# Gating and normalising the probabilities before their transposes, instead of the products after them, in a two-layer attention decoder step

## What is computed

```python
def masked_softmax(logits, valid, sink=None):
    ...
    e = jnp.exp(logits - m)
    den = jnp.sum(e, axis=-1, keepdims=True)
    if sink is not None:
        den = den + jnp.exp(sink - m)
    return e / jnp.where(den > 0, den, 1.0)

def a_finish(x, o, z, gate, w_out):
    n, t = x.shape[:2]
    return x + gate * ((o.reshape(n, t, HD) * jax.nn.silu(z)) @ w_out)

def b_finish(x, o_cmp, o_sel, o_win, z, gl, gate, w_out):
    ...
    mix = jnp.sum(jax.nn.sigmoid(gl)[..., None] * ob * jax.nn.silu(z), axis=2)
    return x + gate * (mix.reshape(n, t, HD) @ w_out)
```

## Time and profile before

| | us |
|---|---|
| runs | 1698.52, 1699.68, 1703.47 |
| median | 1699.68 |
| span of the profiled execution | 1699.8 |
| TensorE matmuls, busy | 1588.0 (93%) |
| VectorE, busy | 934.7 (55%) |
| ScalarE, busy | 613.7 (36%) |
| GpSimd, busy | 485.8 (29%) |

### The profile page before, as it was taken

One profiled execution on the slowest core, in us unless ns is written; L12 is line 12 of the kernel. 1 busy time (PEld: TensorE's weight loads), 2 busy tenths in 40 slices (PEclk: granted clock), 3 DMA queues, 4 the chain that ended last, 5 costly groups with the idle time before them and its releaser, 6 DMA issues.

```text
span 1699.8 us, 31847 instructions
## 1 busy us (share of the span) xinstructions
PE 1588.0 (93%) x11936; PEld 1425.7 (84%) x11936; DVE 934.7 (55%) x2396; ACT 613.7 (36%) x1356; POOL 485.8 (29%) x294
## 2 busy tenths in 40 slices
PE   4579999999699997899999999999999999998997
PEld 1478888888599997788998989989899898886897
DVE  3635555555645415555555755657556575578556
ACT  3413333333214414224434344344443444444112
POOL 0232412221841315355121121211212112149661
PEclk9689999999799997999999999999999999999999
DMA  9233333232612134501021130211101111033732
GB/s 329 92 92 106 106 106 106 107 106 88 236 67 75 47 136 124 141 26 35 15 64 35 29 84 17 88 35 29 35 17 38 35 29 35 18 84 104 255 145 100
DMA packets 82594, 145.16 MB, mean 85 GB/s; under 512 B 19170, under 2 KB 54146, under 8 KB 82274
## 3 DMA queue, kind: packets, MB, share of 16 engines
q1 hardware_dynamic: 69210, 128.64, 23.1%
q10 hardware_dynamic: 10288, 8.46, 1.6%
q0 software_dynamic: 2944, 6.04, 1.3%
HBM read 128.96 MB, written 19.35 MB: 87 GB/s over the span
## 4 chain that ended last, share of the span: by engine, by line
PE 86%; DVE 4%; DMA 3%; ACT 3%; issue 2%; SPq 2%; ACTq 0%; DVEq 0%
PE PS L1032 15%; PE PS L1034 15%; PE PS L1033 15%; PE PS L1287 11%; PE PS L1300 10%; PE PS L1267 5%; PE PS L1268 4%; PE PS L1406 2%; PE PS L1277 2%; DMA WR<-w_ada 2%; PE PS L1229 1%; DMA WR<-sw_v 1%; PE PS L1296 1%; PE PS L1249 1%; PE PS L1382 1%
## 5 line engine op out<-in xcount | busy, mean ns | idle before, releaser
L1032 PE MATMUL PS<-HT_r,WR_r 128*128 128x344 f32 x1344 | 448.8, 334 | 20.0 <-DVE XT_r L1823 15.3
L1034 PE MATMUL PS<-HT_r,WR_r 128*128 128x344 f32 x1344 | 433.4, 322 | 0.0
L1033 PE MATMUL PS<-XT_r,WR_r 128*128 128x344 f32 x1344 | 433.2, 322 | 0.0
L669 POOL TENSOR_TENSOR WR_r<-WR,ONE 128x1024 fp32r<-128x1024 f32 x60 | 116.6, 1943 | 1042.6 <-DMA WR<-w_b 598.3
L1631 ACT ACTIVATE PB<-PB,NM 128x257 f32<-128x257 f32 (+9 forms) x384 | 248.8, 650 | 171.4 <-DVE NM L2023 171.1
L1032 PEld LDWEIGHTS PS<-HT_r,WR_r 128*128 128x128 f32 x1344 | 257.2, 191 | 22.9 <-issue 19.9
L1033 PEld LDWEIGHTS PS<-XT_r,WR_r 128*128 128x128 f32 x1344 | 257.1, 191 | 0.0
L1034 PEld LDWEIGHTS PS<-HT_r,WR_r 128*128 128x128 f32 x1344 | 256.5, 191 | 0.0
L2036 DVE COPY PT<-PS 128x256 f32<-128x256 f32 (+2 forms) x192 | 121.6, 633 | 211.8 <-PE PS L1287 210.7
L1287 PE MATMUL PS<-CST,PB 128*128 128x128 f32 (+1 forms) x1360 | 226.5, 286 | 0.9 <-ACT PT L1639 0.9
L1300 PE MATMUL PS<-PT,VT 128*64 128x128 f32 x2592 | 204.0, 285 | 6.0 <-DVE PT L2036 2.8
(11 more groups left out here) (310 smaller groups left out, 2389.5 us busy)
## 6 DMA issues: line engine op xcount, KB each, us to landing
WR<-w_ada SPq DMA_DIRECT2D x64, 512.0 KB, 5.4
WR<-w_b SPq DMA_DIRECT2D x32, 512.0 KB, 3.3
WR<-w_a SPq DMA_DIRECT2D x17, 512.0 KB, 4.4
STR<-scratch SPq DMA_DIRECT2D x128, 48.0 KB, 1.9
XT<-x SPq DMA_DIRECT2D x8, 516.0 KB, 9.1
HT<-x SPq DMA_DIRECT2D x8, 516.0 KB, 7.2
HT<-x_mid SPq DMA_DIRECT2D x8, 516.0 KB, 5.0
STR<-scratch SPq DMA_DIRECT2D x128, 32.0 KB, 1.9
```

Of the source, the lines that this page charges most:

```text
L669: pool.tensor_tensor(high_r, raw, ONE[:, 0:1].unsqueeze(2).to_broadcast([P, NC, P]), ALU.mult).then_inc(sem("w_split"), 1)
L1032: pe.matmul(out, hw[:, k, :], high, start=(k == 0), stop=False)
L1033: pe.matmul(out, hw[:, k, :], low, start=False, stop=False)
L1034: return pe.matmul(out, lw[:, k, :], high, start=False, stop=(k == NC - 1))
```

## The change

The factor chain goes: `rg`, the transposes of kind "o", `t1`, the tile RG and their semaphores. In its place stands an entry `nr` for each unit and head, behind the two `ex` of the unit. VectorE waits for that exp, takes the reciprocal of the row sum into NM (128x1) and in B multiplies it by the gate. ScalarE then multiplies the probabilities of that unit and head by it in place, with a Copy whose scale is that column of NM. `cmp` is done by VectorE alone, with one multiply of 512 columns. The transposes wait for `nr` where they waited for `ex`. `oe` takes 0.5 times the SiLU gate directly and multiplies the products by it. With the "o" groups gone, even groups always use bank 4 and odd ones bank 5. Waits that stood on `t1` stand on `oe`.

```diff
     for x in units[0]["parts"]:
         emit("ex", x)
+    if phase == "a":
+        for x in units[0]["parts"]:
+            emit("nr", x)
...
     def flush():
-        if late:
-            emit("tr", late)
-            emit("t1", late)
         for g in pending:
...
                 emit("sm", nxt["parts"][1])
-                emit("rg", ending[0])
+                emit("nr", un["parts"][0])
             if early_fill:
                 for x in nxt["parts"]:
                     emit("ex", x)
+                for x in nxt["parts"]:
+                    emit("nr", x)
                 fill(here)
...
-        for hf in ending[0:1] if un["b"] != "cmp" else []:
-            emit("rg", hf)
         emit("tr", gs[0])
         emit("ev", gs[0])
         if nxt and not to_cmp and not early_fill:
             for x in nxt["parts"]:
                 emit("ex", x)
+            for x in nxt["parts"]:
+                emit("nr", x)
         if not early_fill:
             fill(here)
...
-        if un["b"] == "cmp":
-            emit("rg", ending[1])
-            late = ending[1]
-        elif ending:
-            emit("tr", ending[0])
-            emit("t1", ending[0])
...
-            pool.wait_ge(sem("b_t1"), half_index("b", "cmp", PAIRS - 1, 1) + 1)
+            pool.wait_ge(sem("b_oe"), half_index("b", "cmp", PAIRS - 1, 1) + 1)
...
-            sp.wait_ge(sem("a_t1"), plans["a"]["HF"])
+            sp.wait_ge(sem("a_oe"), plans["a"]["HF"])
...
-                        if x["kind"] == "o":
-                            pe.wait_ge(sem(ph + "_rg"), x["h"] + 1)
-                            for i in range(QB // 2):
-                                last = pe.transpose(PS[:, bank, i * P:(i + 1) * P], SS[:, i * P:(i + 1) * P], ident)
-                        else:
-                            un = x["unit"]
-                            pe.wait_ge(sem(ph + "_ex"), un["parts"][-1]["x"] + 1)
...
+                        un = x["unit"]
+                        pe.wait_ge(sem(ph + "_nr"), un["parts"][-1]["x"] + 1)
...
+                    elif what == "nr" and x["unit"]["b"] != "cmp":
+                        un = x["unit"]
+                        sl, at = un["slot"] + x["s"], un["at"]
+                        act.wait_ge(sem(ph + "_rn"), x["r"] + 1)
+                        if ph == "b":
+                            act.wait_ge(sem("b_nr"), x["x"])
+                        p_ = PB[:, sl, at:at + un["keys"]]
+                        scale = NM[:, sl, 2:3] if ph == "a" else NM[:, sl, 3:4]
+                        act.activation(p_, p_, ACT.Copy, scale=scale).then_inc(sem(ph + "_nr"), 1)
...
-            act.wait_ge(sem("b_t1"), plans["b"]["HF"])
+            act.wait_ge(sem("b_oe"), plans["b"]["HF"])
             selected_pages(act, EARLY_PAGES, DEC * PAGES, WR, "sel_v", "sel_v_rest", numbers)
...
+                    elif what == "nr":
+                        un, s = x["unit"], x["s"]
+                        sl = un["slot"] + s
+                        dve.wait_ge(sem(ph + "_ex"), x["x"] + 1)
+                        if un["b"] == "cmp":
+                            c0 = 2 * un["it"]
                             p4 = PB[:, un["slot"], un["at"]:un["at"] + un["keys"]].rearrange("p (q s c) -> p q s c", q=QB, s=2)
+                            den = DEN[:, 0, :, :].rearrange("p s q -> p q s")
                             step(dve.tensor_reduce(den, p4, AX, ALU.add))
                             step(dve.tensor_scalar(den, den, 1.0 / BIG, None, ALU.max))
...
+                            step(dve.reciprocal(den, den))
+                            step(dve.tensor_tensor(den, den, SG[:, :, c0:c0 + 2], ALU.mult))
+                            dve.tensor_tensor(p4, p4, den.unsqueeze(3).to_broadcast([P, QB, 2, NCB]), ALU.mult).then_inc(sem("b_nr"), 1)
                         else:
...
+                            den = DEN[:, BR[un["b"]], s, un["qb"]:un["qb"] + 1]
+                            r = NM[:, sl, 2:3]
+                            if ph == "a":
+                                dve.reciprocal(r, den).then_inc(sem("a_rn"), 1)
+                            else:
+                                c0 = BR[un["b"]] * H + 2 * un["it"] + s
+                                step(dve.reciprocal(r, den))
+                                dve.tensor_tensor(NM[:, sl, 3:4], r, SG[:, un["qb"], c0:c0 + 1], ALU.mult).then_inc(sem("b_rn"), 1)
...
-                            dve.tensor_tensor(out, PS[:, 6, :], SS[:, :], ALU.mult).then_inc(sem(ph + "_oe"), 1)
+                            dve.scalar_tensor_tensor(out, PS[:, 6, :], 0.5, gate, ALU.mult, ALU.mult).then_inc(sem(ph + "_oe"), 1)
                         else:
-                            dve.tensor_tensor(SS[:, :], PS[:, 6, :], SS[:, :], ALU.mult).then_inc(sem(ph + "_oe"), 1)
-                            dve.wait_ge(sem(ph + "_oe"), h + 1)
                             if x["add"]:
                                 dve.wait_ge(sem("b_mix"), x["add"])
+                            dve.scalar_tensor_tensor(SS[:, :], PS[:, 6, :], 0.5, gate, ALU.mult, ALU.mult).then_inc(sem(ph + "_oe"), 1)
+                            dve.wait_ge(sem(ph + "_oe"), h + 1)
                             dve.tensor_tensor(out, out, SS[:, :], ALU.add).then_inc(sem("b_mix"), 1)
```

More of the change, by code:

```diff
@@ L183, in phase_plan @@
         emit("ex", x)
-    pending, late = [], None
+    if phase == "a":
+        for x in units[0]["parts"]:
+            emit("nr", x)
+    pending = []
     def flush():
-        if late:
-            emit("tr", late)
-            emit("t1", late)
         for g in pending:
@@ L231, in phase_plan @@
             flush()
-        late = None
-        for hf in ending[0:1] if un["b"] != "cmp" else []:
-            emit("rg", hf)
         emit("tr", gs[0])
@@ L286, in phase_plan @@
             order.append(x)
-            if x["kind"] == "p":
-                x["c"] = c
-                c += 1
+            x["c"] = c
+            c += 1
     for un in units:
         un["trs"] = max(g["n"] for g in un["groups"]) + 1
+    for r, x in enumerate(x for x in parts_ if x["unit"]["b"] != "cmp"):
+        x["r"] = r
     new = None
@@ L1273, in pairs @@
                         bank = 4 + x["n"] % 2
-                        if x["kind"] == "o":
-                            pe.wait_ge(sem(ph + "_rg"), x["h"] + 1)
-                            for i in range(QB // 2):
-                                last = pe.transpose(PS[:, bank, i * P:(i + 1) * P], SS[:, i * P:(i + 1) * P], ident)
-                        else:
-                            un = x["unit"]
-                            pe.wait_ge(sem(ph + "_ex"), un["parts"][-1]["x"] + 1)
-                            for i, item in enumerate(x["items"]):
-                                if un["b"] == "cmp":
-                                    n, src = 2 * NCB, PB[:, un["slot"], un["at"] + item * 2 * NCB:un["at"] + (item + 1) * 2 * NCB]
-                                else:
-                                    kb, s = item
-                                    n, src = P, PB[:, un["slot"] + s, un["at"] + kb * P:un["at"] + (kb + 1) * P]
-                                last = pe.transpose(PS[0:n, bank, i * P:(i + 1) * P], src, ident)
+                        un = x["unit"]
+                        pe.wait_ge(sem(ph + "_nr"), un["parts"][-1]["x"] + 1)
+                        for i, item in enumerate(x["items"]):
+                            if un["b"] == "cmp":
+                                n, src = 2 * NCB, PB[:, un["slot"], un["at"] + item * 2 * NCB:un["at"] + (item + 1) * 2 * NCB]
+                            else:
+                                kb, s = item
+                                n, src = P, PB[:, un["slot"] + s, un["at"] + kb * P:un["at"] + (kb + 1) * P]
+                            last = pe.transpose(PS[0:n, bank, i * P:(i + 1) * P], src, ident)
                         last.then_inc(sem(ph + "_tr"), 1)
@@ L1910, in add_mask @@
                     step(dve.tensor_tensor(m, m, CST[:, C_FAR:C_FAR + P], ALU.add))
-                def free_sums(h, it, b):
-                    if h:
-                        dve.wait_ge(sem(ph + "_oe"), h)
-                    adds = 0 if ph == "a" else len([x for x in pl["halves"] if "add" in x and x["h"] < h])
-                    if adds:
-                        dve.wait_ge(sem("b_mix"), adds)
                 if ph == "a":
@@ L2036, in pairs @@
                         dve.tensor_copy(PT[0:m, c % 2, 0:n], PS[0:m, 4 + x["n"] % 2, 0:n]).then_inc(sem(ph + "_evd"), 1)
-                    elif what == "rg":
-                        it, b, half, h = x["it"], x["b"], x["half"], x["h"]
-                        un = [u for u in pl["units"] if u["it"] == it and u["b"] == b and u["qb"] in (None, 4 * half + 3)][0]
-                        dve.wait_ge(sem(ph + "_ex"), un["parts"][-1]["x"] + 1)
-                        den = DEN[:, BR[b], :, :].rearrange("p s q -> p q s")
-                        if b == "cmp" and half == 0:
```

(13 more changed lines are left out.)

22 lines of the change are left out of this document (2 added, 20 removed).

## The result

| | before | after |
|---|---|---|
| runs, us | 1698.52 to 1703.47 | 1763.57 to 1770.42 |
| median, us | 1699.99 | 1766.49 |
| span of the profiled execution, us | 1699.8 | 1768.7 |

The ratio is 1.039 (95% interval 1.0369 to 1.041): 66.5 us slower. The prediction was 1725 with a range of 1684 to 1748: slower as forecast, but the loss is 2.6 times as large and outside the range. The profiled execution of the changed kernel is the slowest of its four, 3.9 us above their median.

What follows compares the result with a forecast made beforehand. TensorE bounds full pairs, latency B's last pair. Seven full pairs at +2.65 give +18.5 us; last pair +11, tail +0.7, mixer A -4.6: +25.6, so 1725 us, range 1684 to 1748.

Steps and rivals of the forecast that it cites:

- Factor transposes: Removing 256 TensorE transposes saves 2.8 us a pair of B and 0.7 a pair of A, 28.0 gross.
- (1) cmp: Compressed unit of a full pair: VectorE's longer chain and ScalarE's multiplies delay cmp's eviction and product; 1.36 us lost.
- (2): Unit sel6, with sel7 being prepared: evictions queue behind exp, small operations and multiplies, so TensorE's products wait; 1.1 us lost.
- (3): Unit win0 of a full pair, covered by only a half fill: 0.15 us lost.
- (4): Units win3 and win4: the query copy moves behind two multiplies, making evictions and the next transposes late; 1.55 us lost.
- GpSimd: B's one-column gate multiply waits for GpSimd operations: 1.0 us at win2 to win4 plus 0.3 at sel5, each full pair.
- Rival (d): TensorE's new pauses cost clock, 0.35 us per us of pause, adding 14 us over eight pairs: 1739; chance 0.08.
- (a): Rival: all new work is covered, so the gross 28.0 us saving counts: 1672 to 1692, say 1678; chance 0.22.
- (b): Rival: queues show, but the one-column multiply doesn't wait for GpSimd; +9.6 us, 1709; chance 0.14.
- (c): Rival: savings and stalls cancel, with stalls of 2.2 to 3 us a pair: 1695 to 1705; chance 0.10.
- Last pair: B's last pair, without projections: queued multiplies and evictions cost some 4 us, GpSimd waits 7; +11, ends -2.8 and +25.
- Tail and layer A: Tail: ScalarE's page loads wait for the last sum, +0.7 us. Mixer A: transposes saved, little lost, -4.6 us.

Runs made afterwards that it cites:

- the scalar form: The changed kernel with B's gate multiply taking the gate as one scalar per partition instead of a second tensor: 1747.48 us, ratio 1.0277.
- the last three versions: The changed kernel with compressed-unit order and query copies moved, scalar gate, head 1's multiply later, in three variants: 1703.33, 1706.86 and 1689.79 us.
- a later version: The changed kernel with reordered compressed unit, scalar gate, B's head-1 multiply later, query copies behind the previous branch's output step: 1706.86 us, ratio 1.0037.

## Why the prediction was right in sign and too small

**Factor transposes.** Right: 2.8 forecast, 2.75 measured a pair; 28.0 gross, 29.0 measured.

**Sizes of the new operations.** 640 columns take 0.823 instead of 0.73, 128 take 0.40 instead of 0.35, the first inside its ends; the line through my two rows gives 0.20 for 128, so that the 0.35 had no row. 1024 columns take 1.144, as exp does (1.139), not 1.04: the read of exp's accumulator has a row of its own (0.188), so there was nothing to take off. ScalarE's 22 us a pair are 21.2 (64.01 against 42.85 in the earlier trace rows). VectorE's 0.36 a part holds where nothing waits: 0.163 and 0.159, some 0.31 with the hand-over (two parts from 1096.45 to 1097.07).

**(1) cmp.** The mechanism was right, the size 1.36 was too small: 2.3 by the run that puts the unit first. The rows of VectorE, ScalarE and TensorE there, against the earlier trace rows:

```profile
1092.31 1.96 DVE L2062 TENSOR_TENSOR MT<-MT,SS 128x512 f32<-128x512 f32 x1
...
1095.85 0.69 DVE L2035 TENSOR_TENSOR PB<-PB,DEN 128x512 f32<-128x512 f32 x1
...
1096.84 0.90 ACT L1626 ACTIVATE PB<-PB,NM 128x128 f32<-128x128 f32 x2 [1.83 <-DVE NM L2044]
1097.64 0.78 ACT L1588 ACTIVATE WR<-PS 128x344 f32<-128x344 f32 x2
...
1098.32 0.58 ACT L1633 ACTIVATE PT<-PS 64x512 f32<-64x512 f32 x1
```

ScalarE's queue is the one that I described. VectorE's chain ends 14.0 us after the pair's last cmp score (1096.54 against 1082.5), not 13.1 as I had it. Of the 0.9 us, 0.6 belong to the output step's addition ahead of it. It waits for GpSimd, 1.96 us here and 1.36 in the kernel before, and I had taken that wait as fixed.

**(2), (3) and (4).** (2) 1.1 forecast, 0.44 + 0.68 measured. (3) no pause. (4) 1.55 forecast, 1.10 + 0.60 measured, and the run with the copies moved shows the cause; it gave 2.65 in all.

**GpSimd.** 1.3 a pair forecast, 1.55 by the scalar form (110.75 to 109.2). The small tile does wait; taking L2002 as the nearest row was right. The place was not: I had most of it in win4's pauses, and these are as long in the scalar form (1.15 and 0.55) as in the changed kernel (1.10 and 0.60). Where in a pair the 1.55 lies I can't say beyond 1.0 us of shorter pauses in all, so that the size agrees is in part luck.

**The first pair** isn't like the fourth: +12.1. GpSimd splits other tensors there, and VectorE's two gate multiplies, ScalarE's two multiplies behind them and the compressed unit's eviction behind those all stand in one line:

```profile
753.43 5.30 POOL L696 TENSOR_TENSOR MT_r<-KD,MT_r 64x1024 fp32r<-64x1024 f32 x2
...
754.23 2.11 DVE L2044 TENSOR_TENSOR NM<-NM,SG 128x1 f32<-128x1 f32 x1
...
756.45 2.30 DVE L2044 TENSOR_TENSOR NM<-NM,SG 128x1 f32<-128x1 f32 x1
758.79 0.40 ACT L1626 ACTIVATE PB<-PB,NM 128x128 f32<-128x128 f32 x1 [2.01 <-DVE NM L2044]
...
760.40 1.86 PE L1282 MATMUL PS<-PT,CV 64*128 64x128 f32 x7 [5.16 <-ACT PT L1633]
```

I followed one pair and multiplied by seven.

**The clock** is the step that failed. I had priced it at 0.35 us for each us of pause and set it up as a rival with 0.08, an alternative to a sum made at full clock. It is no alternative: it can come on top of any sum that has pauses in it. So the sum had the clock at nothing, and in the profiles it is 24.7 us, of the 41.5 that the forecast missed by: 14.9 for 48.1 us of new pauses in the full pairs, which is 0.31 for each, and 9.8 for 13.7 in the last pair, which is 0.72. That the first meets my 0.35 is luck: by the profiles of the other kernels each us of new pause in the full pairs cost from 0 (the last three versions) and 0.05 (the compressed unit first) to 0.52 (the scalar form). The runs show that pauses cost clock at certain places, and give no price by their length. Rival (d)'s 1739 is the forecast with that term; it is 10.7 us short of the clock alone (14 against 24.7), because there were 61.8 us of new pauses instead of 40 and because of the last pair's price.

**The sum of the full pairs**, 18.5 forecast and 52.6 measured: 14.9 more is clock, 6.0 the first pair's own net of clock, and 6 x 2.2 = 13.2 the other six, whose pair grew by 4.85 net of clock instead of 2.65 (cmp 0.9 of it; the rest lies in (4) and GpSimd, and perhaps in matmuls that restart behind pauses, which I can't part). That makes 52.6.

**Last pair**: 11 forecast, 19.9 measured, 9.8 of it clock: net of clock 10.1, near the sum, but its parts were not those. The scalar form gives back 9.7, of which 5.1 is clock, so GpSimd's wait is 4.6 where I had 7; leaving ScalarE's multiply out gives nothing net of clock, where I had 4 for its queue. What makes up the other 5.5 no run shows, so that the total agrees is luck.

**Tail and layer A.** The tail's +4.0 can't be laid to the change: of eleven kernels with the same order there, ten had 116.9 to 118.8 us and one 122.7, and the 0.7 forecast can't be seen in that. Layer A's loop gained 5.1 (from its first output step to its last 306.7 us instead of 311.8), 4.6 forecast, but that too is two errors that cancel: without the multiply it takes 302.8 and 302.9 in two runs (clock included in all four), so the gross saving was 8.9 instead of 5.6, and ScalarE's multiply costs 3.8 where I had 1 for the new steps. The rest of the -7.6 lies in stretches that differ between executions of the same code (737.7 to 749.9 us up to B's first pair in ten kernels with layer A as in the changed one).

**The rivals.** (a) is out: three of the four places stalled, for more than the 2.8 us at which it decides, and the pair is longer. (b) is out: the one-column multiply waits. (c) is out. (d)'s sign, a granted clock below 1.00 in full pairs, came (0.97 in the fourth), together with those of the forecast.

## What to carry to other kernels

A step that is moved from the full engine to two half-idle ones costs little by volume and much by place: the same 384 multiplies made the kernel 66 us slower where they stood, and with a few entries of the list moved and one operand form changed the kernel is 0.6% faster than before, although ScalarE is as busy. Before pricing a stall, ask what stands behind the new instruction in each queue, and do so for the first and the last pass of the loop as well as for a middle one. And where a sum puts pauses into an engine that ran at full clock, the clock belongs into the sum as a term with wide ends, not among the rivals.

## What the runs showed of the hardware

- A VectorE multiply of two one-column SBUF tensors waits for GpSimd like a wide one (48 of 256 slow, up to 2.373 us, each ending 13 to 22 ns behind a GpSimd operation); with the second column as a scalar operand none of 256 does (0.212 to 0.218). The Trainium skill, "SBUF — State Buffer", Who interferes with whom, has the rule for two inputs, and this trace agrees down to one element per partition. The Trainium skill, "DVE: scalar operands, raw-bit mode, write accounting and state across instructions", Scalar operands, says that such a scalar does not take up the second tensor stream; that none of these multiplies waited fits it.
- Behind two pauses of 1.1 to 1.5 and 1.2 us with 1 us of work between them (the compressed unit), or of 1.1 and 0.6 us (win4), TensorE ran at 1.2 GHz for 3.4 to 6.8 us, and in the first pair, at pauses of 1.3 and 5.2 us, for 10.2. Whether such a stretch began, and behind which of the two places, differed between pairs with the same pauses. Of pairs 2 to 7, with win4's pauses away, all had one that began at the compressed unit; with that unit's filled with spare work, four had one at win4; with that unit's away, none did, nor did any behind the pauses of 1.2 to 1.4 and 1.2 us, with 1.8 us of work between them, before sel3's scores and sel2's transposes in a later version.
- ScalarE's Copy with a scale column costs what exp costs: 0.823 us for 640 columns, both.
